# First attention of a three-layer block kernel: two groups of heads, and one hand-written order on three engines

## The reference, cut to what matters

```python
down = h @ w_down                                   # 1024 -> 384 + 256 + 64
c_q  = rmsnorm(down[..., :384], q_a_norm)
c_kv = rmsnorm(down[..., 384:640], kv_a_norm)
k_rope = down[..., 640:]
q  = (c_q @ w_uq).reshape(b, s, 8, 192)             # 8 heads: 128 without, 64 with rope
kv = (c_kv @ w_ukv).reshape(b, s, 8, 256)           # 128 of key, 128 of value
k  = concat([kv[..., :128], broadcast(k_rope)])
q, k = rmsnorm(q, q_norm), rmsnorm(k, k_norm)       # over 192, then rope on the last 64
for blk in range(2):                                # 128 queries see 128 or 256 keys
    p = softmax(where(mask, q_blk @ k.T * 192 ** -0.5, neg))
    o_blk = p @ v
x = x + o.reshape(b, s, 1024) @ w_o
h = rmsnorm(x, norm_ffn)                            # then the router and the experts
```

## Time and profile before

| | |
|---|---|
| median of 3 runs | 1398.68 us (1397.64 to 1400.05) |
| the profiled execution | 1395.94 us, of it 1393.9 us span |
| PE matmul busy | 1306.4 us, 94% |
| DVE, ACT, POOL busy | 1045.1, 864.5, 38.9 us |
| mean granted clock of TensorE | 0.968 |

### The profile page before, as it was taken

How to read it: one execution, slowest core, us unless ns; L and a number is a source line. 1 busy time by engine, 2 the same in 40 slices (tenths; PEclk the granted TensorE clock), 3 DMA queues, 4 the chain that set the end, 5 groups by cost and what they waited for, 6 DMA issues and landing times.

```text
span 1393.9 us, 18776 instructions
## 1 busy us (share of the span) xinstructions
PE 1306.4 (94%) x6058; PEld 1067.9 (77%) x6058; DVE 1045.1 (75%) x1471; ACT 864.5 (62%) x1272; POOL 38.9 (3%) x54
## 2 busy tenths in 40 slices
PE   7999999997678999999999999999997975999998
PEld 5878888886556788888888888888886744888887
DVE  4576555565765999999999999999995856555554
ACT  4655444455644687878787878878784544444443
POOL 0000000000300000000000000000000111000000
PEclk9999999998898999999999999999998997999999
DMA  9635555554004597979798888889894410445540
GB/s 359 218 147 199 190 185 181 182 180 151 31 10 172 207 377 303 379 295 382 299 380 327 354 331 344 329 347 366 319 375 157 168 44 1 136 185 193 181 151 31
DMA packets 46121, 319.31 MB, mean 229 GB/s; under 512 B 5152, under 2 KB 6304, under 8 KB 7808
## 3 DMA queue, kind: packets, MB, share of 16 engines
q1 hardware_dynamic: 44288, 316.40, 60.1%
q10 hardware_dynamic: 1680, 2.10, 0.5%
q0 software_dynamic: 112, 0.26, 0.1%
HBM read 316.64 MB, written 2.10 MB: 229 GB/s over the span
## 4 chain that ended last, share of the span: by engine, by line
PE 81%; DVE 11%; issue 3%; ACT 2%; POOL 1%; DMA 1%; DVEq 0%; SPq 0%; ACTq 0%; POOLq 0%
PE bank L349 24%; PE bank L351 24%; PE bank L350 24%; PE bank L645 3%; DVE wl L1231 2%; PE bank L413 2%; DVE x L1645 2%; PE bank L385 1%; DMA fixed<-fixed_dram 1%; PE bank L751 1%; PE bank L580 0%; PE bank L772 0%; PE bank L664 0%; PE bank L665 0%; DVE xtl L1251 0%
## 5 line engine op out<-in xcount | busy, mean ns | idle before, releaser
L1231 DVE TENSOR_TENSOR wl<-raw,wh 128x1024 fp32r<-128x1024 f32 x598 | 714.8, 1221 | 206.0 <-ACT wh L835 194.3
L835 ACT ACTIVATE wh<-raw 128x1024 fp32r<-128x1024 f32 x598 | 631.5, 1061 | 323.1 <-PE bank L351 316.2
L349 PE MATMUL bank<-wh,xth 128*128 128x512 f32 (+2 forms) x1170 | 463.4, 396 | 12.9 <-DVE wl L1231 5.1
L351 PE MATMUL bank<-wh,xtl 128*128 128x512 f32 (+2 forms) x1170 | 454.6, 389 | 0.0
L350 PE MATMUL bank<-wl,xth 128*128 128x512 f32 (+2 forms) x1170 | 454.5, 388 | 0.0
L349 PEld LDWEIGHTS bank<-wh,xth 128*128 128x128 f32 x1170 | 221.5, 189 | 57.8 <-issue 5.3
L351 PEld LDWEIGHTS bank<-wh,xtl 128*128 128x128 f32 x1170 | 221.2, 189 | 46.0
L350 PEld LDWEIGHTS bank<-wl,xth 128*128 128x128 f32 x1170 | 221.8, 190 | 42.3
L349 PE MATMUL bank<-wh,hth 128*128 128x512 f32 x456 | 178.6, 392 | 0.0
L351 PE MATMUL bank<-wh,htl 128*128 128x512 f32 x456 | 178.0, 390 | 0.0
L350 PE MATMUL bank<-wl,hth 128*128 128x512 f32 x456 | 177.4, 389 | 0.0
(11 more groups left out here) (275 smaller groups left out, 794.2 us busy)
## 6 DMA issues: line engine op xcount, KB each, us to landing
raw<-weights_dram SPq DMA_DIRECT2D x299, 1024.0 KB, 4.9
x<-x_dram SPq DMA_DIRECT2D x1, 1024.0 KB, 7.9
bias_scratch<-act ACTq DMA_DIRECT2D x1, 1024.0 KB, 16.0
wide<-bias_scratch ACTq DMA_DIRECT2D x8, 128.0 KB, 2.2
out_dram<-x SPq DMA_DIRECT2D x4, 256.0 KB, 2.1
fixed<-fixed_dram SPq DMA_DIRECT2D x1, 600.0 KB, 8.9
rows<-rows_dram POOLq DMA_DIRECT2D x1, 256.0 KB, 6.3
cols<-cols_dram SPq DMA_DIRECT2D x1, 73.0 KB, 8.6
```

Source lines behind the costliest of these rows:

```text
L349: mm(o, lh, wh[:, wi, sl], start=start, stop=False)
L351: return mm(o, ll, wh[:, wi, sl], start=False, stop=stop)
L835: A(wh[:, c % SPLIT, :], raw[:, (c // 2) % RAW, (c % 2) * UNIT:(c % 2 + 1) * UNIT], ACT.Copy).then_inc(hi_done, 1)
L1231: V.tensor_tensor(wl[:, c % SPLIT, :], raw[:, (c // 2) % RAW, (c % 2) * UNIT:(c % 2 + 1) * UNIT], f32(wh[:, c % SPLIT, :]), ALU.subtract). ...
```

## The change

The eight heads are worked in two groups of four. The columns of `w_uq` and `w_ukv` are sorted for it: a chunk with the rope part of q for all heads (`R0`), then keys, plain q and values of heads 0 to 3 (`KA`, `QA0`, `VA`), then the same for heads 4 to 7 (`KB`, `QB0`, `VB`). Their ten units stay ten. `w_o` is sorted too: unit u holds the rows of one pair of heads and one half of the columns (`WO_UNITS`). Between scores, turned probabilities and values of one head, PE now has a unit of weights: `QB0`, its half unit and `VB` in the first group, `wo` units in the second. Queues of ACT and DVE are written to match.

The arithmetic is moved as well: the low-rank norms are no longer applied before the products (PE turns raw `down`; the norm of the values is applied as ACT copies them, that of q and k is folded into the head norms by `low_scales`); q's rope gain goes into the tables (`trigq`); q's norm is no longer applied to q but as the scale of its scores (`rs` with its sign turned), in `row_max`. Masking, scaling and the row's extreme are one call of `tensor_tensor_reduce` with an accumulator output per 128 queries, where there were a multiply-add, two reductions and a negation. k is scaled straight out of PSUM. Half filled units are split over 512 columns, not 1024 (`HALVED`). Probabilities have one PSUM bank (6) and head outputs share bank 7 by halves.

TensorE after (a core of it; `turn_*` turn four blocks each, `values` waits for the probabilities' copy, `turn_p(h)` for the division of head h):

```diff
-            pe.wait_ge(sem("lora_xn"), 2 * NT)
-            for k in range(5):
...
-            for n in range(7):
...
-            for p, n in enumerate(QK_ORDER):
...
-            for s in range(-1, NH + 2):
...
-            out_proj(U_WO, "ffn1")
...
+            product(U_DOWN + 4, 0, range(0, 4), 192, (bank[5], bank[7]), 0, KD - 1)
+            pe.wait_ge(sem("down_c"), 2)
+            for k in range(4):
+                turn_lora(k)
+            product(U_DOWN + 5, 0, range(4, 8), 192, (bank[5], bank[7]), 0, KD - 1)
...
+            pe.wait_ge(sem("lora_l"), 3)
+            q_chunk(R0, (bank[4], bank[6]))
+            pe.wait_ge(sem("down_c"), 4)
+            turn_lora(4)
+            pe.wait_ge(sem("lora_l"), 5)
+            kv_chunk(KA, (bank[5], bank[7]))
+            q_chunk(QA0, bank[0:2])
+            kv_chunk(VA, bank[2:4])
+            pe.wait_ge(sem("r_c"), 2)
+            turn_q_rope(0, bank[4])
+            turn_q(0, 0, bank[6])
+            kv_chunk(KB, bank[0:2])
+            pe.wait_ge(sem("qkT_a"), 1)
+            turn_q(0, 1, bank[4])
+            turn_k(0, 0, bank[5])
+            turn_k(0, 1, bank[7])
+            pe.wait_ge(sem("qkT_d"), 1)
+            turn_k_rope(0, bank[6])
+            pe.wait_ge(sem("qkT_a"), 3)
+            pe.wait_ge(sem("qkT_d"), 3)
+            scores(0)
+            scores(1)
+            pe.wait_ge(sem("v_c"), 2)
+            product(QB0, 0, (0, 1), WIDE, bank[2:4], 0, 2)
+            turn_p(0)
+            scores(2)
+            values(0)
+            product(QB0 + 1, 0, (2,), WIDE, bank[2:4], 0, 2)
+            turn_p(1)
+            scores(3)
+            values(1)
+            pe.wait_ge(sem("k_ready"), 2)
+            kv_chunk(VB, bank[0:2])
+            turn_p(2)
...
+            scores(4)
+            scores(5)
+            wo(0)
+            turn_p(4)
+            scores(6)
+            values(4)
+            wo(1)
...
+            turn_p(7)
+            wo(4)
+            values(7)
+            wo(6, (0,))
+            wo(5)
+            wo(6, (1,))
+            turn_half("ffn1", 0, 4)
+            wo(7)
```

VectorE after, up to the first scores, and ACT in the first group:

```diff
+            follow(R0, 2, 0)
+            low_scales()
+            r_sums()
+            rotate_q(0, ebuf)
+            follow(KA, 1, 0)
+            k_sums(0)
+            rotate_q(1, hbuf)
+            follow(QA0, 1, 0)
+            k_scaled(0, (bank[5], bank[7]))
+            follow(QA0 + 1, 1, 0)
+            q_sums(0)
+            follow(VA, 1, 0)
+            evac_turned(2, 0, bank[6], "qn")
+            follow(KB, 1, 0)
+            q_scales(0)
+            evac_turned(4, 2048, bank[5], "kn")
+            evac_turned(6, 5120, bank[6])
+            row_max(0)
...
+            exps(2)
+            follow(QB0 + 1, 1, 0)
+            evac_q(1, bank[2:4])
+            copy_p(1)
...
+            follow(VB, 1, 0)
+            evac_v(1, bank[0:2])
+            copy_p(2)
```

```diff
+            def row_max(h):
...
+                for qb, (a, n) in enumerate(((0, P), (P, 2 * P))):
+                    c = 8 * (h // 4) + 4 * qb + h % 4
+                    r = V.tensor_tensor_reduce(out=ebuf[:, b, a:a + n], in0=bank[4 + b][:, a:a + n], in1=maskt[:, a:a + n],
+                                               scale=rs[:, c:c + 1], scalar=3.0e38, op0=ALU.add, op1=ALU.min,
+                                               accum_out=stat[:, 2 * b + qb:2 * b + qb + 1])
```

More of the change, by code:

```diff
@@ L71 @@
 TOTAL = U_END + 2
+R0, KA, QA0, VA, KB, QB0, VB = (U_UQ + n for n in (0, 2, 3, 5, 6, 7, 9))
+HALVED = (R0 + 1, QA0 + 1, QB0 + 1)
+WO_UNITS = ((0, 0), (0, 1), (1, 0), (1, 1), (2, 0), (3, 0), (2, 1), (3, 1))
 DONE_FF1 = NT * (FF1 // FG)
@@ new lines, in _ @@
+            for t in range(NT):
+                sc.wait_ge(sem("r_c"), t + 1)
+                A(xn[:, t, 0:512], act[:, t, 1024:1536], ACT.Square).then_inc(sem("q_sq"), 1)
+            follow(KA, 1, 0)
+            square_k(0, (bank[5], bank[7]))
+            follow(QA0, 2, 0)
+            evac_q(0, bank[0:2])
+            square_q(0)
+            follow(VA, 1, 0)
+            evac_v(0, bank[2:4])
+            evac_turned(1, 4096, bank[4])
+            follow(KB, 1, 0)
+            evac_turned(3, 512, bank[4], "qn")
@@ new lines, in _ @@
+            out_hi(2)
+            copy_p(3)
+            sc.wait_ge(sem("q_red"), 3)
+            evac_turned(9, 1536, bank[0], "qn")
+            out_hi(3)
+            evac_turned(11, 3584, bank[2], "kn")
+            exps(4)
+            exps(5)
+            follow(U_WO, 1, 0)
+            copy_p(4)
+            out_hi(4)
+            exps(6)
+            follow(U_WO + 1, 1, 0)
+            copy_p(5)
+            out_hi(5)
+            exps(7)
+            follow(U_WO + 2, 1, 0)
+            copy_p(6)
@@ L1068, in _ @@
+            squares("ffn1", 1)
+            turned_hi("ffn1", 1, 6)
             rs_ready("ffn1")
@@ new lines, in low_scales @@
+            def low_scales():
+                dv.wait_ge(sem("lora_rs"), 1)
+                mark(V.tensor_scalar(low[:, 2:4], sst[:, 48:50], QH * EPS, None, ALU.mult))
+                mark(V.tensor_scalar(low[:, 0:2], low[:, 0:2], 1.0 / QH, EPS, ALU.mult, ALU.add))
+                for t in range(NT):
+                    r = V.tensor_scalar(kr1[:, t, :], kr1[:, t, :], sst[:, 50 + t:51 + t], rs[:, 50 + t:51 + t], ALU.mult, ALU.mult)
+                    link(r) if t else mark(r)
+                link(V.tensor_tensor(low[:, 0:2], low[:, 0:2], sst[:, 50:52], ALU.mult))
@@ new lines, in _ @@
+            evac_turned(6, 5120, bank[6])
+            row_max(0)
+            k_sums(1)
+            row_max(1)
+            weigh(0)
+            weigh(1)
+            follow(QB0, 1, 0)
+            k_scaled(1, bank[0:2])
+            row_max(2)
+            out_lo(0)
+            follow(QB0 + 1, 1, 0)
+            weigh(2)
+            row_max(3)
+            q_sums(1)
+            out_lo(1)
+            weigh(3)
+            follow(VB, 1, 0)
+            q_scales(1)
+            evac_turned(8, 1024, bank[3], "qn")
```

561 lines of the change are left out of this document (318 added, 243 removed).

## The result

The changed kernel takes 1387.12 us, median of 5 runs (1380.81 to 1391.58); the kernel before took 1400.05 beside it (1397.64 to 1402.27). The ratio is 0.991, with an interval of 0.9889 to 0.9932: faster by 0.9%, 13 us, where 21.5 were forecast, and the median lies 0.1 us above the forecast range of 1371 to 1387. The single runs differ by 10.8 us, and the two lowest times have the two highest mean granted clocks (1380.81 at 0.974, 1385.95 at 0.970; the other three 0.961 to 0.964).

The account below looks back on a forecast made before the run. MLA was taken as a chain to and fro between VectorE, ACT and TensorE, VectorE always late. 23.5 us won, less 0.5 and 1.5, is 21.5: 1374.4 for the profiled execution, 1377.2 for the median, range 1371 to 1387.

Parts of the forecast that it names:

- low-rank part: Start of MLA: `R0` starts at 322.2 without a wait; PE waits 1.1 and starts `KA` at 327.6.
- From KA to the first scores: MLA's products before the scores: VectorE, without a pause, sets the pace until 350.0; PE waits 7.5 us in all.
- The clock: First two heads' scores run partly at half clock, bounds 2.05 and 4.1 each, taken as 3.0 and 2.5: 1.4 us more.
- the sum: MLA stage: 23.5 us won by the projection's end, less 0.5 behind it, less 1.5 for hand-overs: 21.5 us.
- Rival (c): Clock stays low throughout MLA's first group, its 24 us of TensorE work growing by some 15: 1391 us; chance 0.04.
- The row's extreme: New accumulating VectorE operations in each head's `row_max`: 1.0 us a head, bounds 0.7 and 1.5.
- Rival (d): Slower: the accumulating operation is a slow VectorE path on every head's chain; at 5 us a head 1409; chance 0.03.
- First group: Heads 0 to 3: values 1 and 2 wait 1.9 and 1.45 us for ACT; scores 4 begin at 377.7.
- Second group: Heads 4 to 7 and projection: units cover each head's chain, one wait of 0.75 at `wo(5)`; ends at 413.7.
- Behind it: After the projection: turning of x's first half has one unit behind it, not two; 0.5 us charged.
- Rival (a): More waits than walked, on ACT and VectorE in MLA: 14 us won, span 1381 to 1390; chance 0.18.
- (e): No change: the experts give back the time won if they start with fewer units loaded: 1398; chance 0.03.

Follow-up runs that it names:

- the repeat: The changed kernel once more, unedited: 1388.05 us, ratio 0.9928 to the kernel before.
- the trace with the products in both places: Changed kernel plus 5.5 throwaway products ahead of the first scores and those in the second attention's waits: 1371.97 us, ratio 0.9774 to the kernel before.

## Why the prediction was wrong in size and right in kind

- **What bounds the kernel** was read rightly: a chain to and fro, VectorE late. So was the *low-rank part* (`R0` without a wait, `KA` behind a wait of 1.08 for 1.1).
- **From KA to the first scores**: 350.0 + 0.8 walked, 350.95 measured; single waits 0.96, 3.73 and 1.57 for 1.2, 3.75 and 2.5. Right, since VectorE sets the start: the waits are 1.2 us shorter in all, half of it because the last turned lot ahead of the scores took 1.11 at the low clock.
- **The clock** is the step that failed. It charged 1.4 us, "the first two heads' scores run at half the clock in part", with bounds that ended at 4.1 a head and stopped there. Measured 10.7 in the first execution and about 7 in the repeat: the two scores fully (3.4), the unit behind them (2.4), the unit `VB` (1.7), and in the second group scores and a unit (3.2; none in the repeat, but again in the trace with the products in both places). With the clock held up ahead of the first scores the stage took 99.4 us, 22.0 less than before, as the sum has it. Rival (c) had the mechanism and the work at stake, but took all or nothing and got 0.04. The argument against it, that a stretch with a wait of about 1 us in each head stood at 1.00, was one execution's: under the same code and with the turns kept quick, it stood at 0.57. Nor did each head wait so long: the waits there were 0.31, 0.58, 0.96, 0.97 and 0.97, and one head had none.
- The Trainium skill, TensorE: Matmul & The Clock Gate, section "A second HAM failure mode: psum-queue depth-cycling", says of a bf16 kernel that short idles between groups make the clock oscillate. I let one row overrule it; the windows after (0.50, 0.56, then 0.72, then 0.50) and the ones of the kernel before with products side with the page.
- **The row's extreme** was 1.0 us a head with bounds 0.7 and 1.5; it takes 0.76 from start to end, VectorE's timeline after:

```profile
354.78 0.35 DVE L1725 CUSTOM_DVE_ANT_0 ebuf<-bank,fixed,rs 128x128 f32<-128x128 f32 x1 [3.98 <-PE bank L604]
355.06 0.08 DVE L1725 DVE_READ_ACCUMULATOR2_ANT stat<- 128x1 f32 x1
355.06 0.48 DVE L1725 CUSTOM_DVE_ANT_0 ebuf<-bank,fixed,rs 128x256 f32<-128x256 f32 x1
355.46 0.08 DVE L1725 DVE_READ_ACCUMULATOR2_ANT stat<- 128x1 f32 x1
```

  Rival (d) is out. The prediction's comparison on PSUM as a source set a multiply-add beside a row of 420 ns that is a reduction's, so it showed little. Like for like, k's scaling of 512 columns took 688 ns from SBUF and takes 681 out of PSUM (VectorE's groups by form after, 315 to 430 us):

```profile
L1685 DVE TENSOR_TENSOR act<-bank,rs 128x512 f32<-128x512 f32 x4 | 2.6, 681 | 0.0
```

  The Trainium skill, VectorE: DVE Perf Modes, section "The TRN2 errata — SBUF-src ops pay a fixed extra latency per instruction", has PSUM cost more; the trace disagrees.
- **First group**: values 1 and 2 waited 2.19 and 1.54 for ACT (walked 1.9 and 1.45), scores 4 waited 0.83 (0.8). **Second group**: one wait of 0.74 at `wo(5)` (0.75), and each head's chain hidden. Right.
- **Behind it**: the router's first matmul waits 1.33 us for VectorE's low part, but its second wait is 2.40 where it was 2.82. From the last product of the projection to the first of the experts it takes 0.7 us longer; 0.5 was charged. The experts lose another 1.1, for which nothing was charged.
- **Rival (a)** has its number (1381 to 1390 holds 1387.12) and not its mechanism: no wait on the way to the projection was missed, so the match is luck. **(e)**: 1.8 us were given back behind the stage, not the gain.
- The prediction named longer stages behind MLA as a sign that it is wrong, and had no term for them. In the profiled execution the second attention gave back 5.8 us, in part by chance.
- The range failed with the clock's term, 5.6 to 9.3 us too small in a forecast that missed by 8.6. With the clock held up in both kernels, here and in the second attention, the distance is 20.0 us, against a sum of 21.5.

## What to carry to other kernels

A term for the clock belongs to everything that follows a stretch of waits, not only to the first instructions behind it: here two heads' scores and a whole unit of products, 348 to 363.6 us. Price it at both levels, from rows, and keep both in the range. When an order is changed so that TensorE has its work right behind short waits, look at that work's length in the profile before looking for new waits. If the waits can't be removed, throwaway products into a free bank, a little shorter than the wait, cost nothing in these traces (the first scores at 350.95 and 350.96) and brought back what the low clock took. A wait left open later can lose it again: behind one of 2.19 us it fell to 0.79 and to 0.57 from 364 to 372. And look first for what there is to win: where a trace has lost only 3 us to the clock, as the kernel before in this stage, filling all waits brought nothing that the runs can tell.

## What the hardware showed that I had not expected

- With waits of 0.97, 1.46 and 1.62 us between 341.7 and 347.9 and turned blocks between them, TensorE fell to 1.2 GHz (0.66 in the mean from 344 to 364); with the same order and 2.9 us of products in the last two waits it stayed at 2.4 GHz.
- The level in a stretch is not fixed by the program: 388 to 396 stood at 0.50 and 0.72 in one execution and at 1.00 in another of the same kernel. The Trainium skill, TensorE: Matmul & The Clock Gate, section "Loop structure matters more than you think", has the loop nest decide it; here the nest was the same.
- With products in the second attention the changed kernel's runs lay between 1378.68 and 1380.28, without them between 1385.48 and 1391.58. That the scatter comes from there is not shown: with the same products, the kernel before scattered over 6.9 us and the changed kernel with products in both places over 8.7. What picks the places where the clock falls stays open.
